# Down pieces of the expert weights issued from ScalarE's own DMA queue instead of SyncE's

## The reference, cut to what matters

```python
def expert_block(args):
    xblk, e = args
    hid = jax.nn.silu(xblk @ w_gate[e]) * (xblk @ w_up[e])
    return hid @ w_down[e]
```

## Time and profile before

| what | value |
|---|---|
| median of the runs | 1624.23 us (1622.6 to 1625.52, 3 runs) |
| profiled execution, its own time | 1618.63 us |
| profiled execution, span | 1616.8 us |
| TensorE busy | 1514.0 us, 94% of the span |
| ScalarE busy | 299.2 us, 19% |
| mean granted TensorE clock | 0.98 |
| DMA | 484.52 MB, mean 300 GB/s |

### The profile page before, as it was taken

The page is one execution under the profiler, slowest core; times in us unless marked ns, Lnnn a source line. Parts: engine busy times, 40 slices in busy tenths (PEclk is TensorE's granted clock), DMA queues, the critical chain, the costliest instruction groups (busy, mean ns, idle before and its releaser), DMA issues. The chain is left out here.

```text
span 1616.8 us, 21249 instructions
## 1 busy us (share of the span) xinstructions
PE 1514.0 (94%) x7887; PEld 772.9 (48%) x7887; DVE 641.2 (40%) x1656; ACT 299.2 (19%) x755; POOL 83.1 (5%) x143
## 2 busy tenths in 40 slices
PE   9999999999999999989989987869999999999986
PEld 8787877666333333333334444564633333333332
DVE  2656564545324242322333233551523333332324
ACT  2524243213101010000011011361210001010001
POOL 0101010101000000000000000100000000000000
PEclk9999999999999999999999989989999999999998
DMA  6432321639999999999993257504799999999994
GB/s 218 129 109 70 111 70 69 235 110 357 425 426 426 426 426 427 427 426 427 426 392 155 104 189 286 212 1 190 307 425 426 426 426 426 427 426 428 425 425 150
DMA packets 121838, 484.52 MB, mean 300 GB/s; under 512 B 18314, under 2 KB 53038, under 8 KB 73634
## 3 DMA queue, kind: packets, MB, share of 16 engines
q1 hardware_dynamic: 117442, 479.05, 73.6%
q0 software_dynamic: 4320, 4.42, 0.8%
HBM read 483.77 MB, written 10.97 MB: 306 GB/s over the span
## 5 line engine op out<-in xcount | busy, mean ns | idle before, releaser
L2360 PE MATMUL moe_ps_gate<-slots,moe_xrT 128*64 128x512 f32 x1024 | 229.0, 596 | 19.9 <-DMA slots<-in_w_gate_e_dram 19.9
L2360 PE MATMUL moe_ps_up<-slots,moe_xrT 128*64 128x512 f32 x1024 | 226.8, 595 | 0.0
L2388 PE MATMUL moe_ps_y<-slots,router_inputs 128*64 128x512 f32 x960 | 212.6, 595 | 0.0
L2240 DVE TENSOR_TENSOR resid<-resid,moe_ps_x 128x512 f32<-128x512 f32 x60 | 41.3, 688 | 265.2 <-PE moe_ps_x L2404 265.2
L2360 PEld LDWEIGHTS moe_ps_gate<-slots,moe_xrT 128*64 128x64 f32 x1024 | 73.6, 137 | 149.0 <-issue 148.0
L2360 PEld LDWEIGHTS moe_ps_up<-slots,moe_xrT 128*64 128x64 f32 x1024 | 71.3, 137 | 150.8 <-issue 138.7
L907 PE MATMUL gdn_bank<-gdn_xT,slots 128*128 128x288 f32 x512 | 133.0, 409 | 0.7 <-ACT slots L455 0.7
L2388 PEld LDWEIGHTS moe_ps_y<-slots,router_inputs 128*64 128x64 f32 x960 | 66.4, 137 | 124.8 <-issue 124.6
L2031 ACT ACTIVATE moe_xrT<-moe_ps_x,router_inputs 128x128 f32<-128x128 f32 x128 | 36.6, 369 | 379.5 <-PE moe_ps_x L2348 363.9
L907 PEld LDWEIGHTS gdn_bank<-gdn_xT,slots 128*128 128x128 f32 x512 | 93.9, 190 | 24.8 <-issue 1.8
L2209 DVE TENSOR_TENSOR router_inputs<-router_inputs,moe_ps_up 128x512 f32<-128x512 f32 x32 | 22.0, 689 | 195.3 <-PE moe_ps_up L2360 195.3
(11 more groups left out here) (508 smaller groups left out, 1909.9 us busy)
## 6 DMA issues: line engine op xcount, KB each, us to landing
slots<-in_w_gate_e_dram SPq DMA_DIRECT2D x128, 1024.0 KB, 26.1
slots<-in_w_up_e_dram SPq DMA_DIRECT2D x128, 1024.0 KB, 26.5
slots<-in_w_down_e_dram SPq DMA_DIRECT2D x128, 1024.0 KB, 26.4
slots<-in_w_in_a_dram SPq DMA_DIRECT2D x16, 1024.0 KB, 5.5
slots<-in_w_kv_dram SPq DMA_DIRECT2D x4, 2048.0 KB, 17.1
slots<-in_cache_k_dram SPq DMA_DIRECT2D x16, 512.0 KB, 5.0
slots<-in_cache_v_dram SPq DMA_DIRECT2D x16, 512.0 KB, 5.5
slots<-in_state_delta_dram SPq DMA_DIRECT2D x8, 512.0 KB, 7.3
```

The costliest lines, as they stand in the source:

```text
L2240: V.tensor_tensor(half, half, banks[i][:, :], ALU.add).then_inc(s["summed"], 1)
L2360: last = T.matmul(ps[64 * e:64 * e + 64, :], xgT[:, k, 64 * e:64 * e + 64], slots[:, slot[2 * n + e], 512 * k:512 * k + 512], start=(k == ...
L2388: last = T.matmul(ps_y[64 * e:64 * e + 64, h, :], hidT[:, k, 64 * e:64 * e + 64], slots[:, slot[4 + e], 1024 * k + 512 * h:1024 * k + 512 ...
```

## The change

SyncE's `load` now skips the down pieces (p % 6 of 4) up to group 14. ScalarE issues them itself: after the silu of group g it asks for the four halves of the down pieces of group g + 1 in one run, first halves first. It adds no wait of its own, because the silu has already waited for `gate_made`, which says that the old gate pieces are used up. ScalarE's loop of one group becomes three groups written out, two turns of a loop with five groups in its body, and one more group. Group 0's down pieces are fetched ahead as before, and group 15's stay with SyncE.

```diff
             for p in range(SLOT_COUNT, 34, 2):
-                load(p)
+                if p % 6 < 4:
+                    load(p)
             with sp.Fori(0, 2) as j:
                 for p in range(34, 64, 2):
-                    load(p, j)
+                    if p % 6 < 4:
+                        load(p, j)
...
+            def ask_down(g, turns=None):
+
+                for half, landed in ((0, slot_in), (1, slot_in_b)):
+                    for e in range(2):
+                        slot = (6 * g + 4 + e) % SLOT_COUNT
+                        expert = slice(2 * g + e, 2 * g + e + 1) if turns is None else bass.ds(turns * 10 + (2 * g + e), 1)
+                        act.dma_start(slots[:, slot:slot + 1, HALF * half:HALF * half + HALF], W[2][:, expert, HALF * half:HALF * half + HALF]).then_inc(landed[slot], 16)
+
+            def group(g, following=None, turns=None):
+
+                sel_kept(g - 1, flat_hid)
+                silu(g)
+                if following is not None:
+                    ask_down(following, turns)
+                rows_kept(g + 1)
+                kept(g)
+
             rows_kept(0)
             silu(0)
+            ask_down(1)
             rows_kept(1)
             kept(0)
-            with act.Fori(1, LAST) as g:
-                sel_kept(g - 1, flat_hid)
-                silu(g)
-                rows_kept(g + 1)
-                kept(g)
+            for g in range(1, 4):
+                group(g, g + 1)
+            with act.Fori(0, 2) as j:
+                for c in range(5):
+                    group(j * 5 + (c + 4), c + 5, j)
+            group(LAST - 1)
             sel_kept(LAST - 1, flat_hid)
             silu(LAST)
```

## The result

The changed kernel took 1636.27 us, median of 5 runs (1634.05 to 1642.19), against 1622.96 us (1617.07 to 1625.52) for the kernel before. The ratio is 1.009 (95% interval 1.0061 to 1.0119): slower by 13.3 us, 9.9 to 19.3 by the interval. The profiled execution has a span of 1634.6 us, 17.8 more than that of before.

The account below looks back on a forecast made before the run. DMA was taken to bound the expert phases, TensorE close behind. Issues cost 0 us and reordered landing 9.0 us a layer, so 2 x 9.0 = 18 us on 1624.2 gives 1642 us, range 1623 to 1656.

Parts of the forecast that it names:

- The bound and the pace: Expert phases: DMA, saturated near 426 GB/s, needs 30.1 us a group against TensorE's 27.5; the rate stays unchanged.
- The issue times: ScalarE's four issues a group, after the silu: 4.2 us (1.3 to 21.8), costing 0 us.
- the 12 us of cover: ScalarE's 12.3 us between the end of the silu and `rows_kept`, which hides its four issues.
- Equal shares: While both rings hold work, each lands a piece every 5.01 us; equal or near, chance 0.62.
- The wait's place: TensorE waits for up pieces in the up stage's second half, 2 to 3 us a group, until group 13.
- my cross-check: By waits: lead gone 4.5 groups sooner, waits beginning about group 8 in layer 1, 5 or 6 in layer 0.
- The loss by order: The next group's down pieces land among gate and up pieces wanted sooner: 9.0 us lost a layer.
- the sum: Group 15's gate stage ends at + 72.8 instead of + 63.8: 9.0 us a layer, 18 us in both.
- The rivals: Unequal shares, about 1654 to 1659 us (0.13); no reordering that matters, 1622 to 1627 (0.14); faster by bandwidth, 1604 (0.11).

Follow-up runs that it names:

- e9: The change with loops written out, but group 1's down pieces stay with SyncE and ScalarE has groups 2 to 14; +14.1 us over the kernel before.
- e8: The kernel before, with the three stores of normalised rows moved from SyncE to ScalarE's queue, behind its exponentials; -4.7 us against the kernel before.
- e10: The kernel before, with ScalarE issuing each store of normalised rows right behind its normalisation, before the exponentials; -4.6 us against the kernel before.
- e2: The change with loops written out, ScalarE asking for down pieces of groups 1 to 9 only, SyncE for 10 to 14; +4.0 us over the kernel before.
- e3: The change with loops written out, ScalarE asking for down pieces of groups 10 to 14 only, SyncE for 1 to 9; +15.8 us over the kernel before.
- e4: The change, but ScalarE asks only for the first expert's down matrix of each group, SyncE for the second's; +7.3 us over the kernel before.
- e6: The change, but ScalarE asks for the next group's down pieces at the end of its turn; +14.7 us over the kernel before.
- e7: The change itself, groups 1 to 14 by ScalarE, with SyncE's and ScalarE's loops written out; +16.1 us over the kernel before.

## Why the prediction was right

**The bound and the pace: right.** The rate did not move, and a group in the waiting stretch lasts 732.32 - 702.25 = 30.07 us, as in the earlier trace rows. Two queues gave no more bandwidth.

**The issue times: right in what they cost, too high in size.** Four issues took 1.86 us, not 4.2, and cost 0, as the 12 us of cover said.

**Equal shares: shown.** The alternation of landings shows it. That down pieces would land "some 20 us after their issue" holds for the last of four (22.5); the median is 14.3. The Trainium skill's page DMA: Bandwidth & Descriptors (Queues, rings and completion order) has the DMA engines go round the rows that have work; for two hardware queues this case's trace agrees, mostly 4.9 to 5.5 us a piece against 2.44.

**The wait's place: right.** It is in the second half of the up stage, as forecast, until group 13 and with none in the up stage of groups 14 and 15. It begins at group 7 in both layers, where I had 5 or 6 and 8, and lasts 1.9 to 2.0 us a group, where I had 2 to 3. Before, the first wait was in group 10 in layer 0 and group 13 in layer 1, so the lead was gone three and six groups sooner, where my cross-check had 4.5 for both. The late first ask is one group of layer 1's (in e9 its up stages begin to wait in group 8); the rest of the uneven shift I can't explain. Gate stages kept small waits of 0.2 us that I had at none, and one of 1.75 in layer 1's group 14.

**The loss by order: right in kind, one term too large.** The term is the pieces of the next group's down that land ahead of the last up piece: I took 1.6, as if sharing began at the issue. The first piece lands 8.9 us after its issue, and only 0.9 is in by then. The distance grew by 7.9 us a layer, not 9.0. With 0.9 in place of 1.6, the sum gives 9.0 - 0.7 x 2.51 = 7.2 us, so about 0.7 us of the 7.9 is not in it.

**What I had not seen: the late first ask.** I costed the later ask at nothing, since "the late ones of SyncE came 11 us after the gate stage anyway". That cover holds in the waiting stretch, but not at the start of layer 1, where nothing is queued: 2.2 us. Layer by layer, from first gate product to the last down stage, the profiles give +6.9 and +10.3 us, 17.2 in all, against 18 forecast: the order makes 7.9 + 7.9 of it, the layer-1 landing +2.3 and the layer-0 landing -1.0. Most of this -1.0 lies in the starting point: from the start of the span the landing moved only from 836.1 to 835.9, but the first gate product came 0.8 us later (389.70 against 388.90). That 17.2 stands so near 18 is partly luck: the order term was 2.2 us too large, and the late first ask, which I had at nothing, gave 2.3.

**The median.** It came out at 1636.3, below the 1642 forecast. By the medians the difference is 13.3 us, 4.7 less than the 18 of the sum, with an interval up to 19.3. The profiled execution of before is a fast one (1618.6), that of the change is its median, so the profiles' 17.8 probably overstates the loss; and before, run more often, has its median at 1619.6 to 1623.0, below the 1624.2 that I started from.

The rivals fall: the shares are near equal, the order of landing did change, and the bandwidth did not.

## What to carry to other kernels

When DMA is saturated and several kinds of data feed one chain, the order of landing is a schedule. A second queue breaks it: what stands in the shorter queue passes everything in the longer one. So give it what is small and wanted now (the stores of the rows, 4.6 us gained), not what is wanted last (the down pieces, 13 us lost). To judge an order, compare when the last transfer lands with when the work on it ends; if the two are little more than half a stage apart, as here in before, another order has little to give, and what can help is an earlier first ask (e8, e10) or, which no run here tried, fewer bytes. The price of a lag was set by the last groups alone (e2 against e3).

## What the runs showed of the hardware that I had not expected

ScalarE's issues of 1 MiB took 0.34 us each in the median on a queue with room, where I had read 1.06 us a piece from SyncE's run of four in the earlier trace rows. That run is issues at 417.39, 417.76, 420.82 and 421.19: most of its 4.24 us is the wait for the second half of the gate stage, which the merged row hides.

After some idle stretches of TensorE the granted clock dropped to its lower level, 1.2 GHz (0.50 from 1538 to 1540 in e4), and the matmuls behind ran slower. It happened after 3.05 us (6.57 us for sixteen instead of 3.65) and 4.44 us (6.00) in e6, after waits of 2.24 and 2.25 us in e7 (5.29 and 5.35), after 2.78 us in e8 (5.33) and after 1.98 us in e4 (5.35). The length of the one wait does not decide it: other waits of 2.25 us in e7, one of 2.77 us in before (at 1543.74) and all waits of the changed kernel, up to 1.98 us, had 3.65 us behind them. What else decides is open. A wait can thus cost more than its length.
